# Attention value products in groups of eight heads, and all inverse roots on GpSimd, in a two-layer encoder trunk on one core

## What is computed

```python
h = rms_norm(x, g_mix_pre)                       # token mixing
z = h @ w_in                                     # q, k, v of three attentions, forget gates, latents
ya = blocked_attention(A: 8 heads of 64, causal, with cumulated log forget gates)
yb = blocked_attention(B: latents normed and projected up, shared rotary key, mask by chunks of 64)
yc = banded_sink_attention(C: window of two chunks, 8 query heads on 2 key heads, sinks, bias)
merged = ga * (ya @ w_branch_a) + gb * (yb @ w_branch_b) + gc * (yc @ w_branch_c)
x = x + rms_norm(merged @ w_out, g_mix_post)
u = causal_dwconv(rms_norm(x, g_ffn_pre) @ w_up)            # channel mixer
x = x + rms_norm((gelu(u[:2816]) * u[2816:]) @ w_down, g_ffn_post)
pg = sigmoid(rms_norm(x, g_ple_pre) @ w_ple_gate)           # per-layer embedding
x = x + rms_norm(pg * (p @ w_ple), g_ple_post)
```

## Time and profile before

| | us |
|---|---|
| median of 3 runs | 1869.37 (1868.76 to 1870.33) |
| the profiled execution | 1869.82 |
| its span in the profile | 1868.0 |

### The profile page before, as it was taken

One profiled execution on the slowest core, in us unless ns is written; L12 is line 12 of the kernel. 1 busy time (PEld: TensorE's weight loads), 2 busy tenths in 40 slices (PEclk: granted clock), 3 DMA queues, 4 the chain that ended last, 5 costly groups with the idle time before them and its releaser, 6 DMA issues.

```text
span 1868.0 us, 26111 instructions
## 1 busy us (share of the span) xinstructions
PE 1851.1 (99%) x9165; PEld 1529.0 (82%) x9165; DVE 1075.5 (58%) x1925; ACT 861.8 (46%) x1493; POOL 109.1 (6%) x88
## 2 busy tenths in 40 slices
PE   9999999999999999999999999999999999999998
PEld 8887888788888888888898878887888888888886
DVE  4754555545677677325757555655446777773266
ACT  4675546633344444214447744465334444442252
POOL 1000000011001111000000000001110111110000
PEclk9999999999999999999999999999999999999999
DMA  6322363124323333333243223532342333333322
GB/s 176 85 75 80 89 122 96 57 85 169 102 73 97 100 94 97 124 91 101 77 141 92 63 80 108 102 87 67 97 160 89 91 101 91 100 93 121 102 79 79
DMA packets 279589, 183.66 MB, mean 98 GB/s; under 512 B 62500, under 2 KB 262464, under 8 KB 279232
## 3 DMA queue, kind: packets, MB, share of 16 engines
q1 hardware_dynamic: 279112, 182.13, 33.7%
q10 hardware_dynamic: 376, 0.21, 0.1%
HBM read 175.68 MB, written 4.46 MB: 96 GB/s over the span
## 4 chain that ended last, share of the span: by engine, by line
PE 96%; DVE 1%; DMA 1%; ACT 1%; issue 1%; SPq 0%; DVEq 0%; ACTq 0%
PE psum L706 87%; PE psum L881 3%; PE psum L916 2%; PE psum L896 2%; PE psum L746 1%; PE psum L873 1%; PE psum L872 1%; PE psum L893 0%; DMA rx<-rspill 0%; DMA xt<-in_x_dram 0%; ACT xnh L1174 0%; PE psum L718 0%; DVE xt L1600 0%; DVE rtmp L1571 0%; DVE kC L1813 0%
## 5 line engine op out<-in xcount | busy, mean ns | idle before, releaser
L706 PE MATMUL psum<-xnh,wh 128*128 128x512 f32 x1392 | 558.7, 401 | 0.6 <-DVE ub L1863 0.4
L706 PE MATMUL psum<-xnh,wl 128*128 128x512 f32 x1392 | 543.2, 390 | 0.0
L706 PE MATMUL psum<-xnl,wh 128*128 128x512 f32 x1392 | 542.5, 390 | 0.0
L1499 DVE TENSOR_TENSOR wl<-raw,wh 128x1024 fp32r<-128x1024 f32 (+1 forms) x272 | 352.3, 1296 | 281.6 <-ACT wh L1160 281.4
L1160 ACT ACTIVATE wh<-raw 128x1024 fp32r<-128x1024 f32 (+1 forms) x272 | 283.9, 1044 | 372.4 <-PE psum L706 355.4
L706 PEld LDWEIGHTS psum<-xnh,wh 128*128 128x128 f32 x1392 | 261.6, 188 | 57.2 <-issue 8.4
L706 PEld LDWEIGHTS psum<-xnh,wl 128*128 128x128 f32 x1392 | 261.2, 188 | 56.0
L706 PEld LDWEIGHTS psum<-xnl,wh 128*128 128x128 f32 x1392 | 261.9, 188 | 47.8
L1652 DVE CUSTOM_DVE_ANT_0 Sp<-psum,ptok 128x128 f32<-128x128 f32 (+3 forms) x128 | 62.7, 491 | 108.9 <-issue 68.1
L706 PE MATMUL psum<-wh,fh 128*128 128x512 f32 x288 | 112.0, 389 | 0.0
L706 PE MATMUL psum<-wh,fl 128*128 128x512 f32 x288 | 112.0, 389 | 0.0
(11 more groups left out here) (282 smaller groups left out, 2858.0 us busy)
## 6 DMA issues: line engine op xcount, KB each, us to landing
raw<-in_w_up_dram SPq DMA_DIRECT2D x88, 512.0 KB, 3.7
raw<-in_w_gate_dram SPq DMA_DIRECT2D x48, 512.0 KB, 3.8
raw<-in_w_down_dram SPq DMA_DIRECT2D x44, 512.0 KB, 3.5
raw<-in_w_in_dram SPq DMA_DIRECT2D x30, 512.0 KB, 3.8
raw<-in_w_out_dram SPq DMA_DIRECT2D x16, 512.0 KB, 3.6
raw<-in_w_ple_gate_dram SPq DMA_DIRECT2D x16, 512.0 KB, 4.0
rx<-rspill SPq DMA_DIRECT2D x48, 128.0 KB, 2.9
raw<-in_w_in_dram SPq DMA_DIRECT2D x16, 260.0 KB, 2.9
```

Source lines behind the costliest of these rows:

```text
L706: ins = pe.matmul(out, left, right, start=start and n == 0, stop=stop and n == 2)
L1499: dve.tensor_tensor(low[:, 0:n], raw[(L * NCH + c) % RAW][:, 0:n], hi[:, 0:n].bitcast(F32), ALU.subtract).then_inc(w_lo.sem, 1)
```

## The change

Value products:

- Groups of eight units instead of four, at s = 10, 18, 26, 34, in attentions B and C. Attention A has groups of eight for its first two blocks (s = 10 and 18) and groups of four for the last two (22, 26, 30, 34).
- The transposed exponentials lie packed: A's first eight units four to a tile, its next eight two to a tile; C's sixteen in four tiles; B's ring has twelve tiles, eight of them in room that B's inputs held before. `turned_over` names the unit whose products must be done before a slot is written again.

Inverse roots:

- DVE's `inverse_root`, `row_scales`, `inverse_root_of_block` and `root` are gone. GpSimd computes each by an addition of epsilon and a power of -0.5 (`pool.tensor_tensor` with `ALU.pow` and a tile of -0.5). DVE's additions wait for `root_done`. For B's latents DVE still takes the variance out of psum (`variance`), and GpSimd takes its power.
- The factors 1/D, 0.5 and 4 go into the scales of ACT's squares (`YSCALE`, `XSCALE`), B's scale into the variance.

```diff
-GROUP = 4
-RING_PT = {0: 6, 1: 8, 2: 6}
+def products_at(a, s):
+    size = 4 if a == 0 and s > 2 * H + 2 else H
+    return range(s - 2 - size, s - 2, 2) if s % size == 2 and size + 2 <= s <= STEPS + 2 else ()
+
+def turned_over(a, u):
+    if a == 0:
+        if u < 16:
+            return None
+        return {16: 3, 17: 7, 18: 9, 19: 11, 20: 13, 21: 15}.get(u, u - 6)
+    n = 16 if a == 1 else 12
+    return u - n if u >= n else None
...
-YSCALE = math.sqrt(0.5 / D)
+YSCALE = math.sqrt(1 / D)
+XSCALE = [math.sqrt(1 / D), math.sqrt(1 / D), math.sqrt(4 / D)]
...
     def turned_at(a, u):
         if a == 1:
-            return PT[u % 4][:, P * (u // 4 % 2):P * (u // 4 % 2) + P]
-        n = u % RING_PT[a]
-        return PT[n][:, :] if n < 4 else PT_late[a][n - 4][:, :]
+            return PT[u % 4][:, P * (u // 4 % 4):P * (u // 4 % 4) + P]
+        if a == 2:
+            return (PT + PTb)[u % 12][:, :]
+        tiles = PT + th
+        if u < 8:
+            return tiles[u // 4][:, P * (u % 4):P * (u % 4) + P]
+        if u < 16:
+            return tiles[2 + (u - 8) // 2][:, 2 * P * (u % 2):2 * P * (u % 2) + 2 * P]
+        return tiles[(u - 16) % 6][:, :]
...
-            pairs = range(s - GROUP - 2, s - 2, 2) if s % GROUP == 2 and GROUP + 2 <= s <= STEPS + 2 else ()
-            for u in pairs:
+            for u in products_at(a, s):
...
-                if u >= RING_PT[a]:
-                    act.wait_ge(pv_done.sem, pv_done.at(L, n // 2 + (u - RING_PT[a]) // 2 + 1))
+                over = turned_over(a, u)
+                if over is not None:
+                    act.wait_ge(pv_done.sem, pv_done.at(L, n // 2 + over // 2 + 1))
...
         def add(L, n, t, h=0):
             cols = parts(t)[h]
             dve.wait_ge(gained.sem, gained.at(L, done(n, t, h)))
+            dve.wait_ge(root_done.sem, root_done.at(L, TB * n + t + 1))
...
             for t in range(TB - 1):
                 with_gain(L, n, t)
-                root(L, n, t)
                 if t == TB - 2:
                     with_gain(L, n, TB - 1, 0)
                 add(L, n, t)
-            root(L, n, TB - 1)
             add(L, n, TB - 1, 0)
...
     @block.gpsimd
+        def inverse_root(out, x):
+            return pool.tensor_tensor(out, x, half[:, 0:x.shape[1]], ALU.pow)
+        def block_roots(L, n):
+            for t in range(TB - 1):
+                one, w = slice(t, t + 1), rtmp[:, 2, t:t + 1]
+                pool.wait_ge(y_summed.sem, y_summed.at(L, done(n, t)))
+                link(pool.tensor_scalar(w, ysum[:, one], EPS, None, ALU.add))
+                inverse_root(rpost[:, one], w).then_inc(root_done.sem, 1)
+            first, both = rtmp[:, 2, 0:1], rtmp[:, 2, TB - 1:TB]
+            pool.wait_ge(y_summed.sem, y_summed.at(L, done(n, TB - 1, 0)))
+            link(pool.tensor_scalar(first, ysum[:, TB - 1:TB], EPS, None, ALU.add))
+            pool.wait_ge(y_summed.sem, y_summed.at(L, done(n, TB - 1, 1)))
+            link(pool.tensor_tensor(both, ysum[:, TB:TB + 1], first, ALU.add))
+            inverse_root(rpost[:, TB - 1:TB], both).then_inc(root_done.sem, 1)
+        def row_roots(L, n, eps, out, ready):
+            v = rtmp[:, 2, :]
+            pool.wait_ge(x_summed.sem, x_summed.at(L, TB * n + TB))
+            link(pool.tensor_scalar(v, xsum[:, :], eps, None, ALU.add))
+            inverse_root(out[:, :], v).then_inc(ready.sem, 1)
...
         for L in range(DEPTH):
-            pool.wait_ge(x_summed.sem, x_summed.at(L, TB))
+            row_roots(L, 0, EPS, rcol, rcol_ready)
...
+            latent_roots(L)
...
+            block_roots(L, 0)
+            row_roots(L, 1, EPS, rcol, rcol_ready)
...
+            block_roots(L, 1)
+            row_roots(L, 2, 4 * EPS, rhalf, half_r)
+            block_roots(L, 2)
```

More of the change, by code:

```diff
@@ L310, in trunk_kernel @@
     dve_link = sem("dve_link")
+    pool_link = sem("pool_link")
     act_link = sem("act_link")
@@ L352, in trunk_kernel @@
     xsum = nc.alloc_sbuf_tensor("xsum", [P, TB], F32)
+    half = nc.alloc_sbuf_tensor("half", [P, TB], F32)
     rpost = nc.alloc_sbuf_tensor("rpost", [P, TB], F32)
@@ L396, in trunk_kernel @@
     keys_at = [th[0], th[1], PT[0], PT[1]]
-    PT_late = {0: th, 2: [here(f"PTb{i}", 40 + 2 * i, [P, T]) for i in range(2)]}
+    PTb = [here(f"PTb{i}", 40 + 2 * i, [P, T]) for i in range(8)]
     def turned_at(a, u):
         if a == 1:
-            return PT[u % 4][:, P * (u // 4 % 2):P * (u // 4 % 2) + P]
-        n = u % RING_PT[a]
-        return PT[n][:, :] if n < 4 else PT_late[a][n - 4][:, :]
+            return PT[u % 4][:, P * (u // 4 % 4):P * (u // 4 % 4) + P]
[7 more added lines that the diff above has]
+        return tiles[(u - 16) % 6][:, :]
     ytok = here("ytok", 108, [P, T])
@@ L1515, in pre_norm_lo @@
                                          ).then_inc(xn_lo.sem, 1)
[L1517 to L1551, removed]
@@ L1553, in scale_rows, with variance @@
+        def variance(L, norm):
+            i = AUXI["cs" + norm]
+            by = BSCALE ** 2 if norm == "q" else 1.0
+            dve.wait_ge(aux_full.sem, aux_full.at(L, i + 1))
+            dve.tensor_scalar(rtmp[:, RB_VAR.index(norm), :], aux_bank(L, i)[:, 0:TB], 1.0 / (NORM_D[norm] * by), EPS / by,
+                              ALU.mult, ALU.add).then_inc(aux_empty.sem, 1)
+            dve.wait_ge(aux_empty.sem, aux_empty.at(L, i + 1))
+            dve.sem_inc(var_ready.sem, 1)
         def scale_rows(L, norm, dst):
@@ L1557, in scale_rows @@
             dve.wait_ge(aux_empty.sem, aux_empty.at(L, i + 1))
[L1559 to L1570, removed]
-                link(L, dve.scalar_tensor_tensor(out=a, in0=r, scalar=r, in1=w, op0=ALU.mult, op1=ALU.mult))
-                link(L, dve.scalar_tensor_tensor(out=r if n < 2 else rpost[:, one], in0=a, scalar=-1.5, in1=r,
-                                                 op0=ALU.add, op1=ALU.mult))
         def gate(L, t, h=0):
@@ L1591, in with_gain @@
                               ).then_inc(gained.sem, 1)
-        def root(L, n, t):
-            dve.wait_ge(y_summed.sem, y_summed.at(L, done(n, t)))
-            inverse_root_of_block(L, t)
         def add(L, n, t, h=0):
@@ L1624, in embedded @@
                 with_gain(L, 2, t)
-                root(L, 2, t)
                 add(L, 2, t)
@@ L1630, in embedded @@
             with_gain(L, 2, TB - 1, 1)
-            root(L, 2, TB - 1)
             add(L, 2, TB - 1, 0)
@@ L1643, in attention @@
                     dve.wait_ge(bias_in.sem, bias_in.at(L, bias_in.per))
+                if s == 0 and a == 2:
+                    dve.wait_ge(rq_ready.sem, rq_ready.at(L, 1))
                 if s == 0 and a == 0:
@@ L2029, in _, with link, latent_roots @@
     def _(pool):
+        links = [0]
+        def link(ins):
+            links[0] += 1
+            ins.then_inc(pool_link, 1)
+            pool.wait_ge(pool_link, links[0])
+        def inverse_root(out, x):
[17 more added lines that the diff above has]
+            inverse_root(out[:, :], v).then_inc(ready.sem, 1)
+        def latent_roots(L):
+            pool.wait_ge(var_ready.sem, var_ready.at(L, 1))
+            link(inverse_root(rq[:, :], rtmp[:, 0, :]))
+            pool.tensor_scalar(nrq[:, :], rq[:, :], -1.0, None, ALU.mult).then_inc(rq_ready.sem, 1)
+            pool.wait_ge(var_ready.sem, var_ready.at(L, 2))
+            inverse_root(rcol[:, :], rtmp[:, 1, :]).then_inc(rcol_ready.sem, 1)
         pool.memset(Pr[0][:, :], 0.0).then_inc(zeros_set, 1)
+        link(pool.memset(half[:, :], -0.5))
         pool.memset(rpost[:, 0:1], 0.0).then_inc(f_lo.sem, 1)
```

14 lines of the change are left out of this document (7 added, 7 removed).

## The result

The changed kernel takes 1860.47 us (median of 5 runs, 1859.11 to 1861.48) against 1869.37 for the kernel before, a ratio of 0.9949 with a 95% interval from 0.9934 to 0.9964. The forecast was 1859.9. The execution that was profiled took 1860.8 us, 9.0 less than the profiled one of before (1869.82); its span is 1859.0 us, 9.01 less.

What follows compares the result with a forecast made beforehand. TensorE, busy 1851.1 of 1868.0 us, was taken as the bound. From 1869.82, 7.0 for fewer groups and 2.9 for roots on GpSimd gave 1859.9 us; the 8-in-10 range was 1858.0 to 1864.5.

Steps and rivals of the forecast that it cites:

- The price of a group: Value products on TensorE: each group costs 0.35 us beyond its products, whatever its size; 20 fewer groups save 7.0 us.
- The rival that the price belongs to the products: Value products: the 0.35 us is not the change of shape, long groups pay it again inside; 1866.9 us, chance 0.03.
- Nothing given back: Attention stages: larger groups make nothing late; cost put at nothing, from 0 to 2 x 0.35 us for each A stage.
- The rival of half of part one: Attentions: longer stretches without products return half the groups' 7.0 us as TensorE waits for ACT; 1863.4 us, chance 0.10.
- The chain of the root: From last sum of squares to additions: 0.76 us on GpSimd instead of 1.76 on DVE, 1.0 us saved.
- the rival's 1.4 us: GpSimd's power alone takes about 1.4 us, as dear as DVE's chain, so roots gain nothing; 1862.8 us, chance 0.15.
- the 3.5 at which the sum would have turned: Root on GpSimd: the whole change turns slower once sum of squares to additions passes 3.5 us; slower rival's chance 0.05.
- The end and the joint of the layers: Kernel end and first layer to second: the faster root saves 1.0 us and 0.9 us.
- Output projection to channel mixer: Joint occurring twice: 0.5 us saved each, 1.0 in all, next limit the copy of the first transposed tile.
- TensorE's share of 0.2: Joint behind the output projection: lower bound of the saving, transposes starting at 511.6 instead of 511.77; DVE's is 1.0.
- Channel mixer to embedding: Joint occurring twice: root hidden behind `ple`, cover of 6.0 us, so nothing gained or lost.
- part two: Inverse roots moved from DVE to GpSimd: 1.0 + 0.9 + 1.0 = 2.9 us saved at four places.

Runs made afterwards that it cites:

- groups_alone: Changed kernel's eight-head groups and packed slots with inverse roots left on DVE, against the kernel before: 1862.65 us, ratio 0.9960.
- groups_of_two: Kernel before with a value-product group for each pair of units, 96 groups instead of 48: 1885.91 us, ratio 1.0089.
- idle_narrow: Changed kernel plus two idle 64-column products in each of 58 steps of attention C without a group: 1889.96 us, one run.
- joints_shorter: Changed kernel with DVE's gain multiplication and a ScalarE sum of squares moved earlier, idle transposes cut to 20 and 8: 1859.48 us, ratio 0.9944.
- sums_first: Changed kernel with DVE's reciprocal of attention A's last sums and its transfer put ahead of C's two key copies: 1858.04 us, ratio 0.9941.
- whole_again: The changed kernel run once more without edits, beside other runs, compared with the kernel before: 1860.22 us, ratio 0.9960.
- roots_alone: Kernel before with only the inverse roots moved to GpSimd, groups of four and old slots kept: 1869.51 us, ratio 0.9996.
- power_twice: Changed kernel with GpSimd's power of each sub-layer's last block taken twice, one waiting for the other: 1863.85 us, one run.
- idle_wide: Changed kernel plus one idle 128-column product in each of 58 steps of attention C without a group: 1874.59 us, one run.
- roots_again: Kernel before with only the inverse roots on GpSimd, the same kernel run a second time: 1867.75 us, ratio 0.9992.

## Why the prediction was right, and where it was off

- **The price of a group, right.** 0.35 us was forecast, 7.0 for twenty. The stages of the changed kernel lost 1.32 in A and 2 x 2.84 in C and B, 7.00 us; `groups_alone` gives 0.35 and `groups_of_two` 0.36. The rival that the price belongs to the products falls with the chain's rows of 32, 48 and 64 records and with `idle_narrow`.
- **Nothing given back, right.** The groups' own savings are whole in both stages; no wait of TensorE on ACT or on a copy appeared in them beyond the two of the 0.45 us that were there before. The rival of half of part one is out.
- **The chain of the root, half right.** It was to take 0.76 us and takes 1.10. The power was mis-sized: 0.57 us, not 0.40; the addition is 0.19 for 0.15 and the hand-overs 0.34 together for 0.21. The rate of a 512-column addition says nothing of the first column of a power. 0.66 us was saved where I wrote 1.0. The power is still far below the rival's 1.4 us, and the chain below the 3.5 at which the sum would have turned.
- **The end and the joint of the layers, off by that term alone.** 0.67 and 0.66 for 1.0 and 0.9: with 0.66 in the chain, all of it arrives, as the prediction said of both places.
- **Output projection to channel mixer, the limit right, the size by luck.** 0.46 each for 0.5. The prediction named the next limit, the copy of the first transposed tile, and TensorE's share of 0.2 (0.25 measured), but then took the middle between the shares without working it out. The copy follows the transposes and comes 0.30 us earlier, and the rest part had stood 0.16 behind what the copy allowed (513.02 - 512.13 = 0.89 us behind the copy's start before, 0.73 now): 0.46, which is all that any chain shorter by that much or more would have given. `joints_shorter` agrees: with four idle transposes fewer it is 0.37 more.
- **Channel mixer to embedding, right.** 0.00, and 0.00 even with the power doubled.
- **Two terms were missing, and cancel little.** The wait at the start of C came out 0.64 us longer in one layer and 0.50 shorter in the other; the start of the kernel 0.13 longer. So the sum is -7.00 - 2.25 + 0.14 + 0.13 = -8.98 of 9.01. The forecast was -9.9, and the 0.9 us between them are nearly all the chain's 0.34 at two places (0.57 together) and these two terms.

The wait at the start of C was in the trace of before, 1.5 us in two waits, and the prediction's first question, where TensorE stands still, should have listed it. It would not have changed the sum, since neither part touches its cause, but it is where `sums_first` found 2.2 us in the medians, about what part two brought in the traces (2.25).

## What to carry to other kernels

Where TensorE is the bound, look for what it pays at each change of the shape of its products: the idle time of the load queue that no engine releases, counted by groups, gives the number, and the distances around a group give its price, here 0.35 us whether the group has four records or sixty-four. Small chains on another engine pay only where TensorE stands still or is finished, and there the next limit must be read too (here idle transposes and a copy behind them), since it keeps part of what the chain gives. Read every wait of the bounding engine, short ones too: a reordering of a few lines at two such waits was worth 2.2 us in the median, about as much as the roots that changed engines brought in the traces.

## What the runs showed of the hardware that was not expected

- GpSimd's power costs 0.57 us for one column and 1.02 to 1.04 for four, but 1.59 in two of ten, at the same place of either layer (that of B's second latents; why stayed open). The additions beside it cost 0.19 to 0.25. Four columns cost nearly twice what one does, so the price isn't the entry alone.
- TensorE's clock is lost in single executions, at places that differ. Windows of the changed kernel and, below, of the same kernel in `whole_again`, from before the first pass:

```profile
8.35:15.18 6.83, 6.53 (x28) 4.75 (x26) 3.40 (x6) 3.53 (x6) 0.00 (x0) 0.50 0.79 271
```

```profile
8.35:15.18 6.83, 4.62 (x30) 3.46 (x31) 4.01 (x7) 4.23 (x8) 0.00 (x0) 1.00 0.73 246
```

  The first pass came at 14.74 us in the one and at 14.11 in the other. Where the stretch of lower clock reached well into the first passes it cost from 0.7 to 1.4 us (`roots_alone`, `power_twice`, `joints_shorter`, `idle_wide`, `roots_again`), and 0.2 where it ended within the first (the changed kernel, 0.43 us between the first two passes instead of 0.23); where it ended before them, nothing (`groups_alone`, `groups_of_two`). TensorE waits there for the input, from memory. What decides it in a given execution stayed open. For a comparison of one or two microseconds it means that one profiled execution is not enough, and that its start has to be compared by itself.
- The landing of one and the same transfer varies. Over the 48 transfers of the sums (`rx` from `rspill`, 128 KB each) in the changed kernel, from issue to landing:

```profile
DMA to landing us min/median/max: 2.8/2.9/3.9
```

  At the start of C, TensorE's wait hangs on such a landing, and it was from nothing to 2.09 us over the profiled executions. An edit that touches nothing there still seems to gain or lose a microsecond in a single trace.
